# Two of eight token tiles by a dense pass over all experts, in a mixture kernel that gathers expert rows

## The reference

```
n = rmsnorm(h);  u, v, o, i, f, q, k, vs = split(n @ w_in)
h = h + concat(mlstm(u, v, o, i, f), stick_breaking_attention(q, k, vs)) @ w_out
n = rmsnorm(h)
for each of 8 heads:                       # 128 x 128 = 16384 experts
    s = (n @ w_query) . sub_keys           # two lists of 128 scores
    16 best of each list, 256 pair sums, 16 best pairs -> expert numbers, softmax g
    act = gelu(n . expert_u[number])       # 16 dot products of width 1024 for each token
    h += sum(g * act * expert_v[number])
out = rmsnorm(h[128:])
```

## Time and profile before

| | |
|---|---|
| median of 3 runs | 3465.17 us (3459.03 to 3474.46) |
| profiled execution, span from first to last instruction | 3457.6 us |
| PE / PEld busy | 63% / 33% |
| DVE busy | 62% |
| GpSimd busy | 57% |
| ACT busy | 19% |
| mean granted TensorE clock | 0.766 of full speed |
| moved by DMA | 1160.93 MB, mean 336 GB/s |

### The profile page before, as it was taken

The page is one execution under the profiler, slowest core; times in us unless marked ns, Lnnn a source line. Parts: engine busy times, 40 slices in busy tenths (PEclk is TensorE's granted clock), DMA queues, the critical chain, the costliest instruction groups (busy, mean ns, idle before and its releaser), DMA issues.

```text
span 3457.6 us, 32843 instructions
## 1 busy us (share of the span) xinstructions
PE 2170.6 (63%) x10776; PEld 1129.7 (33%) x10776; DVE 2140.8 (62%) x5482; ACT 648.4 (19%) x1393; POOL 1980.4 (57%) x2079
## 2 busy tenths in 40 slices
PE   7999999646654567555654567456763677444433
PEld 6888644223221232123221333123321343111110
DVE  5652665567666666657675666666765766665563
ACT  2221232112211121102210222103310232100000
POOL 0000366776666666666566656666666556666665
PEclk9999999867776677767876778767885787666656
DMA  6103799999999999999999899999999989999998
GB/s 233 46 24 129 257 350 363 390 369 366 355 385 375 366 370 358 387 365 358 349 389 371 338 361 341 389 362 367 366 396 368 343 322 359 365 368 368 369 370 320
DMA packets 335778, 1160.93 MB, mean 336 GB/s; under 512 B 36916, under 2 KB 41720, under 8 KB 335608
## 3 DMA queue, kind: packets, MB, share of 16 engines
q0 software_dynamic: 294912, 1073.87, 81.9%
q1 hardware_dynamic: 40696, 84.95, 6.8%
HBM read 1140.83 MB, written 17.84 MB: 335 GB/s over the span
## 4 chain that ended last, share of the span: by engine, by line
PE 27%; issue 19%; POOL 18%; another core or an unknown queue 14%; DVE 12%; DMA 6%; ACT 3%; SPq 0%; DVEq 0%; POOLq 0%; ACTq 0%
POOL work L914 9%; POOL work L898 9%; PE xs L1728 8%; PE xs_ahead L1728 8%; PE acc L1728 6%; DVE work L1602 5%; PE bank L1728 5%; DMA work<-expert_u,chosen 3%; DMA work<-expert_v,idx_v 2%; DVE work L1256 1%; DMA weights<-w_out 1%; DVE work L1248 1%; ACT L1142 1%; DVE rest L1501 0%
## 5 line engine op out<-in xcount | busy, mean ns | idle before, releaser
L898 POOL DMA_INDIRECT work<-expert_u,chosen x1024 | 984.9, 962 | 736.3 <-DVE chosen L1256 347.1
L914 POOL DMA_INDIRECT work<-expert_v,idx_v x1024 | 990.5, 967 | 725.5 <-remote 299.1
L1602 DVE CUSTOM_DVE_ANT_0 work<-work,xs 128x1024 f32<-128x1024 f32 x875 | 1053.9, 1218 | 395.3 <-DMA work<-expert_u,chosen 240.8
L1728 PE MATMUL acc<-work,lw 128*32 128x512 f32 x4096 | 772.1, 823 | 610.9 <-DMA work<-expert_v,idx_v 449.6
L1728 PEld LDWEIGHTS acc<-work,lw 128*32 128x32 f32 x4096 | 143.7, 134 | 1060.8 <-issue 544.6
L1728 PE MATMUL bank<-weights,n2T 128*128 128x256 f32 x1024 | 262.4, 410 | 10.4 <-issue 10.1
L1728 PEld LDWEIGHTS bank<-weights,n2T 128*128 128x128 f32 x1024 | 205.1, 206 | 123.6 <-issue 95.6
L1602 DVE CUSTOM_DVE_ANT_0 work<-work 128x1024 f32<-128x1024 f32 x128 | 156.2, 1227 | 112.8 <-DMA work<-expert_u,chosen 100.3
L1728 PE MATMUL xs_ahead<-work,neg_tri 128*128 128x512 f32 (+1 forms) x176 | 136.2, 867 | 135.7 <-issue 59.5
L1728 PE MATMUL xs<-work,weights 128*128 128x128 f32 x1472 | 176.5, 282 | 0.0
L2029 PE MATMUL bank<-ident,w_spread 128*128 128x128 f32 x64 | 25.5, 398 | 237.3 <-ACT idx_v L933 154.7
(11 more groups left out here) (232 smaller groups left out, 2541.1 us busy)
## 6 DMA issues: line engine op xcount, KB each, us to landing
work<-kv_dram SPq DMA_DIRECT2D x72, 256.0 KB
work<-expert_u,chosen POOLq DMA_INDIRECT x1024
work<-expert_v,idx_v POOLq DMA_INDIRECT x1024
weights<-w_in SPq DMA_DIRECT2D x6, 2048.0 KB, 19.3
mix_dram<-work SPq DMA_DIRECT2D x34, 256.0 KB, 2.4
weights<-w_out SPq DMA_DIRECT2D x4, 2048.0 KB
weights<-w_queryT SPq DMA_DIRECT2D x4, 2048.0 KB, 12.4
kv_dram<-work SPq DMA_DIRECT2D x18, 256.0 KB, 2.5
```

Source lines behind the costliest of these rows:

```text
L898: pool.indirect_dma_start(out=ring[:, s, :], out_offset=None, in_=expert_u, in_offset=bass.IndirectOffsetOnAxis(ap=chosen[:, G % KEPT_HEAD ...
L914: pool.indirect_dma_start(out=ring[:, s, :], out_offset=None, in_=expert_v, in_offset=bass.IndirectOffsetOnAxis(ap=idx_v[:, G % PH, col:co ...
L1602: nc.vector.tensor_tensor_reduce(ring[:, row, :], ring[:, row, :], rows, 1.0, 0.0, ALU.mult, ALU.add, dots[:, d:d + 1]).then_inc(dotted, 1)
L1728: return nc.tensor.matmul(out_, lhsT, rhs, start=start, stop=stop, skip_group_check=True)
```

## The change

Tiles 4 and 6 are no longer gathered. `PASSES` lists the six tiles that are; the slots become 6 x 128 + 32.

- **Selection** stays for all 64 heads (`ROUTED`). For a head of tile 4 or 6 `choose` makes, in place of the gather indices, cell numbers (expert x 256 + token), and `invert` scales the softmax weights. GpSimd adds those weights into a table in DRAM (`w_dram`, 16384 experts x 256 tokens, 16.8 MB) by 256 indirect transfers of 128 numbers each (`scatter`), one in each of the slots 269 to 524, each ahead of the slot's two gathers. The table is zeroed in the front by 16 stores of 1 MB (`zero_w`).
- **Dense pass.** In slots 536 to 759 come 128 blocks of 128 experts, four in seven slots. For each block SP loads 0.5 MB of U (a transposed copy of the table, `u_blocks`), 0.5 MB of V and, for every four blocks, 0.5 MB of the weight table. TensorE multiplies the block's U with both tiles (`dense_z`: 8 matmuls of 256 columns), ScalarE takes the GELU (`gelu_d`), VectorE multiplies by the weights (`mult_d`), and TensorE adds the product with V into `xs` and `xs_ahead` (`dense_out`: 4 matmuls of 512 columns, two blocks later). Both stand ahead of `sum_set` in the slot.
- **Mixing** of tiles 3 to 8 follows a tighter order (`FAST_STEPS`, `FAST_TAIL`): it starts at slots 112, 176, 240, 304, 368 and 435 and ends at 507, and heads 8 to 63 are selected every 7 to 9 slots or so, from slot 109 to 563.
- **Buffers.** The dots read the tile's rows from two buffers in SBUF, filled through DRAM (`store_rows`, `load_rows`), and no longer from PSUM; U rows have 6 buffers and V rows 8, from U gather 570 and V gather 560 on 10 and 16. Residuals are stored in DRAM after mixing and loaded again for each pass (`store_h`, `load_pass_h`).
- Semaphores of single steps are shared (`Step` for `Lp`, `Lg`, `Lt` and others), with the same waits.

```diff
-RING_U = 7
-RING_V = 10
-HEADS = LAST * PH
+PASSES = [1, 2, 3, 5, 7, 8]
+DENSE = [4, 6]
+GT = len(PASSES)
+RING = 16
+ROWS_AT = (12, 13)
+EXTRA = 12
+HEADS = GT * PH
+ROUTED = LAST * PH
...
+PICKED_HEADS = 16
+FAST_STEPS = {"now": 0, "qk": 1, "copy_qk": 2, "kw": 3, "se": 3, "exp_w": 4, "p": 5, "hh": 6, "inter": 7, "nd": 8,
+              "dstate": 8, "skip": 9, "h": 9, "mean": 10, "rstd": 10, "hn": 11, "hn_t": 12, "ym": 13, "blocks": 14}
+PERIODS = {1: 8, 2: 8, 3: 8, 4: 7, 5: 6, 6: 5, 7: 5, 8: 5}
+MIX_EACH = 64
+MIX_AT = {2: 14, 3: 112}
+for _M in range(3, TILES):
+    MIX_AT[_M + 1] = MIX_AT[_M] + max(MIX_EACH, FAST_STEPS["blocks"] + (_M + 1) * PERIODS[_M] + FAST_TAIL["rows"])
...
+D_STEPS = N_BLOCKS = 128
+DENSE_AT = 536
+DENSE_LAG = 2
+DENSE_SLOTS = 224
+D_U, D_V, D_W, D_G, W_EACH = 4, 4, 2, 3, 4
+D_TOKENS = len(DENSE) * P
+ZEROS = 16
...
+V_RINGS = [(0, [8, 9, 10, 11, 14, 15]), (55, [6, 8, 9, 10, 11, 14, 15]), (63, [7, 6, 8, 9, 10, 11, 14, 15]),
+           (560, [16, 17, 18, 19, 20, 21, 22, 23, 7, 6, 8, 9, 10, 11, 14, 15])]
+U_RINGS = [(0, [0, 1, 2, 3]), (36, [4, 0, 1, 2, 3]), (61, [5, 4, 0, 1, 2, 3]), (570, [24, 25, 26, 27, 5, 4, 0, 1, 2, 3])]
...
+def dense_at(j):
+    return DENSE_AT + j * DENSE_SLOTS // D_STEPS
...
+def scatters_at(s):
+    for d in range(len(DENSE) * PH):
+        r = (DENSE[d // PH] - 1) * PH + d % PH
+        first = scores_at((DENSE[d // PH] - 1) * PH) + 26 + TOPK * (d % PH)
...
+            def zero_w(c):
+                n = N_BLOCKS * D_TOKENS // ZEROS
+                sp.dma_start(w_rows[:, c * n:(c + 1) * n].rearrange("i (r n) -> i r n", n=P * 4),
+                             lw[:, :].unsqueeze(1).broadcast_to([P, n // (P * 4), P * 4])).then_inc(w_zeroed, 16)
...
+            def load_u_d(j):
+                wait(sp, z_d_done, j - D_U + 1)
+                sp.dma_start(u_d[j % D_U], u_blocks[j]).then_inc(first_u_in[j % D_U], 16)
+            def load_v_d(j):
+                wait(sp, out_d_done, j - D_V + 1)
+                sp.dma_start(v_d[j % D_V], expert_v.rearrange("(i j) d -> i j d", j=N_BLOCKS)[:, j, :]).then_inc(
+                    first_v_in[j % D_V], 16)
+            def load_w_d(g):
+                if g == 0:
+                    sp.wait_ge(scattered, 16 * len(DENSE) * PH * TOPK)
+                wait(sp, g_d_ready, W_EACH * (g - D_W + 1))
+                n = W_EACH * D_TOKENS
+                sp.dma_start(w_d[g % D_W].rearrange("p j t -> p (j t)"), w_rows[:, g * n:(g + 1) * n]).then_inc(
+                    first_w_in[g % D_W], 16)
...
+            def scatter(d, k):
+                if k == 0:
+                    if d == 0:
+                        pool.wait_ge(w_zeroed, 16 * ZEROS)
+                    pool.wait_ge(cell_ready, d + 1)
+                    pool.wait_ge(gate_d_ready, d + 1)
+                    wait(pool, scattered, 16 * TOPK * d)
+                pool.indirect_dma_start(out=w_cells, out_offset=bass.IndirectOffsetOnAxis(
+                                            ap=cell[:, d % PH, k:k + 1], axis=0),
+                                        in_=gate_d[:, d % PH, k:k + 1], in_offset=None, compute_op=ALU.add
+                                        ).then_inc(scattered, 16)
...
+                for d, _, c in scatters_at(s):
+                    scatter(d, c)
...
+            def gelu_d(j):
+                act.wait_ge(z_d_done, j + 1)
+                wait(act, out_d_done, j - D_G + 1)
+                nc.scalar.activation(g_d[j % D_G], bank[6][:, 0:D_TOKENS], ACT.Gelu).then_inc(
+                    gelu_d_ready, 1)
...
+            def mult_d(j):
+                TT(g_d[j % D_G], g_d[j % D_G], w_d[g % D_W][:, j % W_EACH, :], ALU.mult).then_inc(g_d_ready, 1)
...
+            def dense_z(j):
+                pe.wait_ge(first_u_in[j % D_U], 16 * (j // D_U + 2))
+                wait(pe, gelu_d_ready, j)
                 for k in range(KC):
+                    last = mm(bank[6][:, 0:D_TOKENS], u_d[j % D_U][:, k, :],
+                              n2T_d[:, k, :, :].rearrange("p a t -> p (a t)"), k == 0, k == KC - 1)
+                last.then_inc(z_d_done, 1)
+            def dense_out(j):
+                pe.wait_ge(g_d_ready, j + 1)
+                pe.wait_ge(first_v_in[j % D_V], 16 * (j // D_V + 2))
+                for a in range(len(DENSE)):
+                    for n in range(2):
+                        last = mm((xs, xs_ahead)[a][:, n, :], g_d[j % D_G][:, a * P:(a + 1) * P],
+                                  v_d[j % D_V][:, n * 512:(n + 1) * 512], j == 0, j == D_STEPS - 1)
+                last.then_inc(out_d_done, 1)
...
+                    for j in dense_steps(at):
+                        dense_z(j)
+                        if j >= DENSE_LAG:
+                            dense_out(j - DENSE_LAG)
                     v = 4 * (I - STREAM) + o // SET - V_LAG
...
                     if o % SET == 0 and 0 <= v < SETS:
                         sum_set(v)
```

More of the change, by code:

```diff
@@ L339, in part, with slot @@
             return work[:, a:b]
-        ring = work[:, 0:(RING_U + RING_V) * D].rearrange("p (s d) -> p s d", s=RING_U + RING_V)
+        ring = part("ring").rearrange("p (s d) -> p s d", s=RING)
+        extra = weights[:, 0:EXTRA * D].rearrange("p (s d) -> p s d", s=EXTRA)
+        def slot(i):
+            return ring[:, i, :] if i < RING else extra[:, i - RING, :]
         arena = part("arena")
@@ L370, in program @@
         tri = take(P)
+        W36 = TILES * MH
+        gate_rows_sb = [take(P)[0:MH, :] for _ in range(6)]
+        lf, tmp4, f_cols = take(MH), take(MH), take(MH)
+        m_row = take(TILES + 1)[0:MH, :]
+        dec_row = take(TILES)[0:MH, :]
+        dec_blk = take(MH)[0:MH, :]
         assert cut[0] <= 4 * D
@@ L761, in _ @@
             sp.dma_start(subT[:, :, :], sub_t).then_inc(late_in, 16)
+            zeroed = 0
             for kind, what in ITEMS:
+                if kind == "unit" and what in UNITS_A[4:] and zeroed < ZEROS:
+                    if zeroed == 0:
+                        sp.wait_ge(fills, FILLS)
+                    zero_w(zeroed)
+                    zeroed += 1
                 if kind == "square" and what == 5:
@@ new lines, in _ @@
+                for q in range(2, GT + 1):
+                    T = PASSES[q - 1]
+                    if s == max((q - 2) * SLOTS + 2, MIX_AT[T] + tail(T, "rows") + 3):
+                        load_rows(q)
+                    if s == (q - 1) * SLOTS + OUT_AT + 2:
+                        store_y(q - 1)
+                        load_pass_h(q)
+                if s == MIX_AT[LAST] + tail(LAST, "rows") + 3:
+                    begin_dense()
+                    load_dense_h(0)
+                if s == DENSE_AT - 1:
+                    for g in range(D_W):
+                        load_w_d(g)
@@ L1119, in copy_n2T @@
                 wait(act, scores_done, PH * (T - 1))
+                wait(act, n2T_stored, 16 * sum(1 for t in DENSE if t < T))
                 for k in range(KC):
@@ L1193, in mixing @@
                     copy_n2T(M)
+                if n == tail(M, "rows") and 1 < M and M in PASSES:
+                    copy_rows(M)
             for kind, what in ITEMS:
@@ L2073, in mixing @@
                     n2_t(M)
+                if n == tail(M, "rows") and 1 < M and M in PASSES:
+                    n2_rows_ahead(M)
             square_sums(0)
```

737 lines of the change are left out of this document (433 added, 304 removed).

## The result

The changed kernel takes 3607.81 us (median of 4 runs, 3601.13 to 3629.85) against 3462.59 us (4 runs, 3459.03 to 3474.46): the ratio is 1.039 (95% interval 1.034 to 1.045). The change makes the kernel 4% slower, where the prediction had it 1.4% faster. The profiled execution has a span of 3607.9 us.

The account below looks back on a forecast made before the run. It took the DMA engines' gathers as the bound, GpSimd second. Stretches of 705 + 512 + 998 + 34 + 1098 + 23 + 40 gave a 3410 us span, plus 7.6 us: 3418 us, 8-in-10 range 3270 to 3620.

Parts of the forecast that it names:

- scatter stretch: Slots 269 to 525, one scatter each: GpSimd becomes the bound at 3.9 us a slot, 998 us in all.
- the three stretches: Slots 109 to 269, slots 269 to 525 with the scatters, and the dense part, slots 536 to 760.
- Up to slot 269: Old work up to slot 109, 705 us, then slots 109 to 269 at 3.2 us each, 512 us.
- I take a gather's price: Slots 269 to 525: a scatter costs GpSimd what a gather does, 1.25 us; bounds 0.3 and 2.5 us.
- rival 1: Slots 269 to 525: a scatter costs GpSimd more than a gather; at 1.9 us each, 3584 us; chance 0.22.
- the rule stated with it: Chance of faster: half of the forecast's 0.35, plus Rival 3 and the case of every cover holding; stated as 0.47.
- Rival 2: Slots 109 to 525 and dense part: the short V ring sets the pace, 3604 us; chance 0.16.
- Rival 3: Scatters are cheap and the DMA engines stay the bound, 2.95 us a slot in the scatter stretch, 3154 us; chance 0.12.
- The dense stretch: Slots 536 to 760 with the 128 blocks: TensorE and DMA level, 4.9 us a slot, 1098 us.
- the turns and waits: Dense part, per slot: turns add about 0.1 us to TensorE's work; waits between groups raise 4.72 to 4.9 us.

## Why the prediction was wrong

- **What bounds the kernel.** Right. GpSimd was named as the second limit with 0.4 us of slack a slot, and the scatter stretch as the place where it takes over. The adding of scatters alone to the kernel before moved its pace by just this. Of U gathers per 100 us it forecast 31, 26 and 20 for the three stretches, where 31, 20 and 23 came; the DMA share of 0.8 in the scatter stretch and TensorE's full clock in the dense one came as forecast.
- **Up to slot 269.** 1241 us against 1217. The 3.2 us a slot of slots 109 to 269 was nearly right (540/167 = 3.23). Most of the missing 24 us lies before: 102 gathers were out at 700 us, not 108. The rings are shorter there, but no run tests that as the cause.
- **Slots 269 to 525: the step that failed**, in the words of the prediction "I take a gather's price". GpSimd as the bound was the right mechanism; its term was too small. The scatter measured 2.03 us with its waits, not 1.25 (+200 us), inside the bounds of 0.3 and 2.5 but above the 1.45 from which rival 1 decides. Rival 1 came true, and so did its sign, a scatter row above 1.1 us busy. That its 3584 us lie within 1% of the result is in part luck: the other misses, +115 and -41 us in this stretch, +24 before it and -98 behind it, cancel. The writes in place of adds show why: 1.0 us for a write, 1.62 for an add. The argument for rival 1 that it "also reads and adds in DRAM" pointed there, and the argument against it, steady work per index, holds for writes alone. The chance given to a slower kernel was 0.40. (The 0.47 for a faster one adds up to only 0.175 + 0.12 + 0.15 = 0.445 by the rule stated with it.)
- **A term that the sum lacked.** That the dots now read the rows from SBUF stood in the change's description and was priced at nothing. It stretched the gathers by some 0.2 us each, which is most of the +115 us: 91 of them went with the rows in PSUM. The sign was in the rows: 214.83/200 = 1.07 us a gather in 352 to 700 us of the earlier trace rows, where tile 1's dots read SBUF, against 264.13/280 = 0.94 us in 3000 to 3400. I had read neither as a price. The traces and the two kernels with SBUF rows agree with a rule of the Trainium skill (SBUF — State Buffer, "Who interferes with whom"): a VectorE instruction with two inputs in SBUF contends with a GpSimd instruction that reads SBUF, through a port pair that works as an exclusive lock. The instruction in question is the gather's, whose row numbers lie in SBUF. By an estimate from the rows above, a gather held up for a whole dot would come to 0.94 + 1.23 = 2.17 us; the one in the timeline took 1.97.
- **Rival 2, the short V ring.** Not in the scatter stretch of the changed kernel, where waits for V sums are 3.0 us in all; one ring place less costs the kernel before 0.6%. It does bind once GpSimd is sped up: 126 us of waits without scatters, 187 with PSUM rows and writes (66 of them with no releaser on record).
- **Rival 3.** It took the scatter for cheap, and the scatter is not. Without any the time is 3215 us, not 3154, and a slot takes 3.4 us, not 2.95, at a DMA share of 0.91 and with the 126 us of waits for V sums: by the prediction's own reading of the earlier trace rows that is the rings' pace and not the DMA engines'.
- **The dense stretch.** 98 us better than forecast from slot 525 on, with TensorE as the bound, as forecast. A block's two products were sized right: 3004.88 to 3008.44 us for the first (3.56, forecast 3.62) and 2999.50 to 3003.03 for the second (3.53, forecast 3.52). The V set is shorter (1.85 us from start to start, forecast 2.14), and the turns and waits, 0.1 and 0.18 us a slot, did not come: TensorE is busy 936.30 of 940 us. By these sizes a slot takes TensorE 4/7 x 7.09 + 1.85/4 = 4.51 us. The U gathers show 4.37, as GpSimd gets ahead of TensorE: the last dense product, begun at 3572.52 us and 1.88 us long, ends 23 us behind the start of the last U gather.

```profile
2999.50 1.88 PE L2038 MATMUL xs<-work 128*128 128x512 f32 x4
3001.22 1.88 PE L2038 MATMUL xs_ahead<-work 128*128 128x512 f32 x4
3003.03 1.92 PE L2038 MATMUL acc<-weights,lw 128*32 128x512 f32 x16
3004.88 3.72 PE L2038 MATMUL bank<-weights 128*128 128x256 f32 x16
3008.44 1.88 PE L2038 MATMUL xs<-work 128*128 128x512 f32 x4
```

```profile
L1152 POOL DMA_INDIRECT work<-expert_u,chosen x688: 932/979/2526, 351.0 to 3551.6; - x172
```

- **The order in TensorE's program.** The prediction gave it nothing, and it is nothing (3608.12 to 3607.81 us).

Where did the gain go? The 256 slots taken away were worth 765 us. The dense pass takes 224 x (4.37 - 2.99) = 309 us of that, the scatter stretch 1270 - 256 x 2.99 = 505, and the first 269 slots 70 (1241 us, where by the earlier trace rows 279 U gathers were out at 1200, so 269 at some 1171). That is 119 of the 150 us by which the span grew. Another 16 lie behind the last U gather (3607.9 - 3551.6 = 56 us, where it was 40), while TensorE ends its dense products; the rest I have not placed. The 505 are GpSimd's: 392 us came back without the scatters, and 79 with the dots' rows in PSUM. A version that beats the kernel before was not found. The nearest one that computes the same is that with PSUM rows, 2% slower.

## What to carry to other kernels

Price a new kind of transfer on the engine that issues it, and take a row of a plain one only for a plain one: with an add, 128 four-byte numbers cost GpSimd 1.62 us, more than a half-megabyte gather. When a change moves the bound to another engine, every small cost on that engine that was hidden before is due, so look in the old trace for the durations that differ between stretches. And a sum of two savings holds only until the next wait: taking both GpSimd costs down gave no more than one. To see what an edit is worth, compare the stretch that it touches: of 39 us that one run seemed to gain, 37 lay ahead of the first edited instruction.

## What the runs showed of the hardware

- An indirect transfer of 128 rows of 4 KB and an indirect write of 128 numbers of 4 bytes take GpSimd nearly the same time (medians 0.94 and 0.995 us); an indirect add of 128 numbers takes 1.62 us, in two different kernels.
- Dots with both inputs in SBUF stretch a gather's mean from 0.96 to 1.10 and 1.13 us on GpSimd, with no effect on the time while the DMA engines are the bound.
- With three software transfers (two gathers, one write) every 3.8 us and no pause, TensorE, VectorE and ScalarE stood still together for 12 to 19 us at a time, until GpSimd stopped. With a wait for the landed write in each slot this was gone, and the stretch took the same time. The way this comes about is open.
- The kernel before ran three times at 3197 us on one occasion and at 3431 to 3488 us on all others. That is open too.
